# Gate and up weights of the experts read in runs of eight rows per partition, gathered x taken from every eighth column

## The reference, cut to what matters

```python
h = jax.nn.silu(jnp.einsum('td,edf->tef', xf, w_gate)) * jnp.einsum('td,edf->tef', xf, w_up)
y = jnp.einsum('tef,efd->td', h * gates[:, :, None].astype(h.dtype), w_down)
```

## Time and profile before

| | us |
|---|---|
| median of 3 runs | 989.9 (989.45 to 990.78) |
| the profiled execution, its own time | 992.38 |
| its span, first to last instruction | 990.7 |

### The profile page before, as it was taken

The page is one execution under the profiler, slowest core; times in us unless marked ns, Lnnn a source line. Parts: engine busy times, 40 slices in busy tenths (PEclk is TensorE's granted clock), DMA queues, the critical chain, the costliest instruction groups (busy, mean ns, idle before and its releaser), DMA issues.

```text
span 990.7 us, 14556 instructions
## 1 busy us (share of the span) xinstructions
PE 959.4 (97%) x5530; PEld 818.1 (83%) x5530; DVE 727.5 (73%) x905; ACT 561.3 (57%) x629; POOL 37.8 (4%) x79
## 2 busy tenths in 40 slices
PE   8999989999999999999999999899999999999997
PEld 7978988888888779878888788679887788888886
DVE  4888885988898774645988888756565977777566
ACT  3845652577777644563677667624553756656441
POOL 8000010100000000001000000000000000000010
PEclk9999998999999999999999999999999999999999
DMA  9833336299989945431599899745452566555711
GB/s 321 278 111 128 128 100 199 79 323 356 306 302 359 357 155 186 160 96 43 170 339 342 274 352 359 256 128 185 157 191 85 183 201 205 175 175 203 250 52 42
DMA packets 151985, 205.82 MB, mean 208 GB/s; under 512 B 6896, under 2 KB 123376, under 8 KB 151920
## 3 DMA queue, kind: packets, MB, share of 16 engines
q1 hardware_dynamic: 150912, 204.24, 61.4%
q10 hardware_dynamic: 1008, 0.71, 0.2%
HBM read 203.87 MB, written 1.05 MB: 207 GB/s over the span
## 4 chain that ended last, share of the span: by engine, by line
PE 79%; DVE 10%; issue 4%; ACT 4%; DMA 2%; SPq 1%; POOL 0%; POOLq 0%; DVEq 0%; ACTq 0%
PE psum L638 77%; DVE w_lo L1961 3%; ACT w_hi L1493 1%; ACT arena L1493 1%; DMA raw<-in_a_w_in 1%; DMA raw<-in_attn_w_in 1%; DVE stats L2225 1%; SPq L281 1%; DVE x_res L2245 1%; PE psum L1117 1%; DVE x_res L2238 1%; DVE xt L1978 0%; ACT mt_hi L1493 0%; PE psum L1368 0%; DVE mt_lo L1978 0%
## 5 line engine op out<-in xcount | busy, mean ns | idle before, releaser
L1961 DVE TENSOR_TENSOR w_lo<-raw,w_hi 128x2048 fp32r<-128x2048 f32 x184 | 418.1, 2287 | 71.6 <-ACT w_hi L1493 69.8
L1493 ACT ACTIVATE w_hi<-raw 128x2048 fp32r<-128x2048 f32 (+1 forms) x186 | 353.9, 1905 | 105.0 <-PE psum L638 43.7
L638 PE MATMUL psum<-xt,w_hi 128*128 128x256 f32 (+1 forms) x1056 | 253.6, 321 | 3.8 <-DVEq L2709 1.7
L638 PE MATMUL psum<-xt,w_lo 128*128 128x256 f32 x704 | 197.1, 280 | 0.0
L638 PEld LDWEIGHTS psum<-xt,w_hi 128*128 128x128 f32 x1056 | 177.1, 190 | 20.3 <-issue 2.7
L638 PE MATMUL psum<-w_hi,mt_hi 128*128 128x512 f32 (+1 forms) x448 | 174.1, 389 | 0.2 <-issue 0.2
L638 PE MATMUL psum<-w_hi,mt_lo 128*128 128x512 f32 (+1 forms) x448 | 171.3, 382 | 0.0
L638 PE MATMUL psum<-w_lo,mt_hi 128*128 128x512 f32 (+1 forms) x448 | 171.0, 382 | 0.0
L638 PEld LDWEIGHTS psum<-xt,w_lo 128*128 128x128 f32 x704 | 133.6, 190 | 0.0
L638 PE MATMUL psum<-w_hi,xt 128*128 128x512 f32 (+1 forms) x368 | 115.2, 385 | 8.0 <-ACT mem_v L1493 3.7
L638 PEld LDWEIGHTS psum<-w_hi,mt_lo 128*128 128x128 f32 x448 | 84.2, 188 | 16.7
(11 more groups left out here) (252 smaller groups left out, 1024.1 us busy)
## 6 DMA issues: line engine op xcount, KB each, us to landing
raw<-in_w_gate SPq DMA_DIRECT2D x64, 512.0 KB, 4.9
raw<-in_w_up SPq DMA_DIRECT2D x64, 512.0 KB, 6.1
raw<-in_w_down SPq DMA_DIRECT2D x64, 512.0 KB, 6.0
raw<-in_ffn_w_up SPq DMA_DIRECT2D x44, 512.0 KB, 4.6
raw<-in_a_w_in SPq DMA_DIRECT2D x26, 512.0 KB, 6.9
raw<-in_attn_w_in SPq DMA_DIRECT2D x24, 512.0 KB, 5.9
raw<-in_ffn_w_down SPq DMA_DIRECT2D x22, 512.0 KB, 4.0
raw<-in_w_o SPq DMA_DIRECT2D x16, 512.0 KB, 4.6
```

Source lines behind the costliest of these rows:

```text
L638: return pe.matmul(o, l, r, start=start, stop=stop, skip_group_check=skip)
L1493: return act.activation(o, i, f, **kw)
L1961: return dve.tensor_tensor(w_half(h, w_lo), w_half(h, raw), w_half(h, w_hi).bitcast(F32), ALU.subtract).then_inc(lo_split, 1)
```

## The change: what it does

It changes two things, which belong together. The view of the gate and up weights becomes `(p k)`: partition p now holds rows 8p to 8p + 7, and a half takes four of them, which lie side by side in memory, 4 KB of gate and 4 KB of up. The place in `raw` to which each row goes stays as it was (1 KB, then a gap of 1 KB). So chunk k now holds the rows k, k + 8, k + 16 and so on, and the stationary operand of the gather takes the same features: column k of each run of eight, 128 numbers of 4 bytes that lie 32 bytes apart, instead of 128 numbers side by side. The transposes in the branch `dense` change in the same way. Number, shapes and order of all instructions and all bytes moved stay the same.

```diff
-                wg = a["w_gate"][layer].rearrange("(g j) (k p) f -> g j p k f", j=PER_GROUP, p=P)
-                wu = a["w_up"][layer].rearrange("(g j) (k p) f -> g j p k f", j=PER_GROUP, p=P)
+                wg = a["w_gate"][layer].rearrange("(g j) (p k) f -> g j p k f", j=PER_GROUP, p=P)
+                wu = a["w_up"][layer].rearrange("(g j) (p k) f -> g j p k f", j=PER_GROUP, p=P)
...
+        def every_eighth(v, b, k):
+
+            return v[:, b, :].rearrange("p (m k) -> p k m", k=KC)[:, k, :]
...
-                                last = mm(o, x[:, b, P * k:P * k + P], perm[:, b, :],
+                                last = mm(o, every_eighth(x, b, k), perm[:, b, :],
...
-                            last = pe.transpose(again(b)[:, k // 4, k % 4, :], x_res[:, b, P * k:P * k + P], ident[:])
+                            last = pe.transpose(again(b)[:, k // 4, k % 4, :], every_eighth(x_res, b, k), ident[:])
```

## The result

| | before | after |
|---|---|---|
| first timing, median of four executions each, us | 989.81 | 1011.14 |
| ratio, 95% interval | | 1.0197 [1.0177, 1.0218] |
| the profiled execution, us | 992.38 | 1008.75 |
| its span, us | 990.7 | 1007.0 |

The four executions after took 1008.75, 1008.88, 1013.4 and 1913.76 us; the last one was disturbed and is left out of the ratio, but not of the median of four (the other three have their median at 1008.88). The change made the kernel 2.0% slower, from 1.8 to 2.2%. 1001.8 was forecast, with a range up to 1006.5.

What follows compares the result with a forecast made beforehand. TensorE was taken as the bound, DMA close behind with 1.4 us (4%) margin a group. Reads 0, gather +11.9, transposes 0 made 1002.6 on the span, 1001.8 us at the median; range 986.5 to 1006.5, the forecast's own 997 to 1006.5.

Steps and rivals of the forecast that it cites:

- The gather: Four gathers, 128 spread loads: 0.218 us each, between ends 0.109 and 0.458; +12.5 us, less 0.6 hidden, +11.9.
- some 300 was the sign named: Sign of being right: gather weight loads (tile perm over xt) near 0.3 us recorded instead of 0.19.
- two waits on `perm_t`: First gather of each layer: some 0.3 us of waiting hides part of the slower loads, twice 0.3.
- the 1.13 us of issue stays: Branch behind a layer's first gather: its 1.13 us of instruction issue follows the gather and isn't hidden.
- pass over the whole 4 KB: Upper end for a gather load: TensorE passes over all 4 KB, 0.458 us, +43.3 us; as rival 1033 us, chance 0.06.
- The line of 16 bytes: Gather loads, by the skill's SBUF cachelines: 0.229 us a load, some +14 us less 0.6; set beside the sum, not used.
- The read of gate and up weights, costed at 0: Expert weight transfers: packets stay 1 KB at 350 GB/s, cost 0; bounds from a 3.1 us gain to +9.6 us.
- a sign of being wrong: Expert groups of 37 us, with ScalarE waiting for w_up throughout, would show the forecast wrong.
- mirrored: Gate and up reads: 4 KB runs in memory only, taken to behave like runs in `raw` only, no gain.
- The witness itself: Third layer's up weights, 1 KB rows in memory, 4 KB runs in `raw`: 1 KB packets at 339 GB/s.
- The rival of slower transfers: Gate and up reads 8 KB apart fall under 330 GB/s; at 10% slower +9.6, 999.5 us with free loads; chance 0.05.
- The dense transposes, order and queues: Dense-branch transposes don't run, cost 0; SyncE issues the same DMAs after the same waits, group margin unchanged.

Runs made afterwards that it cites:

- e7: e4's dense reads with gate and up rows each in 4 KB runs in `raw`, gather as in the kernel before; 992.75 us, ratio 1.0006.
- e1: The kernel before with only the gather's spread weight loads, weights read as before (features don't match); 1005.38 us, ratio 1.0138.
- f1: e1 timed again, beside f2 and f3: the kernel before with the spread gather alone; 1006.23 us, ratio 1.0145.
- e5: The kernel before with its four gathers taking weights 8, 12, 16 and 20 bytes apart (sums changed), one execution; 1000.1 us.
- e2: The kernel before with only the `(p k)` reads of gate and up weights, gather as before (features don't match); 993.73 us, ratio 1.0021.
- e4: As e2, but a half takes rows 512 h + 4p to 4p + 3, so partitions' 4 KB runs join without holes; 991.02 us, ratio 0.9997.
- f4: The changed kernel with sorting moved into the `x_hi`/`x_lo` copies; gather reads neighbours, `start_sums` reads at 512-byte steps; 999.49 us, ratio 1.0075.
- f3: The whole changed kernel timed a third time, beside f1 and f2; 1009.35 us, ratio 1.0173 to the kernel before.
- f2: e2 timed again, beside f1 and f3: the kernel before with the `(p k)` reads alone; 995.02 us, ratio 1.0032.
- after_again: The changed kernel timed a second time, unaltered, beside the kernel before; 1008.72 us, ratio 1.0188.
- e3: e2 with gate rows and up rows each side by side in `raw`, so both transfer sides have 4 KB runs; 993.21 us, ratio 1.0025.

## Why the prediction was wrong

*What bounds it.* Right. TensorE's own time set the stage; e7 lets weights come earlier than before, and nothing is gained. That the DMAs are close behind was right as well, and it is what the cost of the reads comes from.

*The gather.* Right in mechanism, sign and place, short in size. The spread load was put at 0.218 us, the middle in ratio of two ends; it measures 0.245 (recorded 337 ns; some 300 was the sign named), so the term was 128 x 0.125 = +16.0 instead of +12.5. Taken off it was 0.6 for two waits on `perm_t`; the trace of before has only one of them, 0.3 us, and that went under as said. That "the 1.13 us of issue stays" failed: with the longer gather the issue behind it is hidden in the changed kernel, in both layers, 2.2 us (in e1 and f1 0.56 and 0.54 us of it are left). 16.0 - 0.3 - 2.2 = 13.5 us; the marks of the trace have 12.9, the ratios of e1 and f1 13.7 and 14.4. These errors together moved the sum by under 2 us. The upper end of that term, "pass over the whole 4 KB", falls with e5: the price stops rising at 16 bytes.

*The line of 16 bytes.* The sentence that the prediction set beside its sum gave 0.229 us a load and some +14 us. That was nearer than the middle of the two ends: measured are (7.73 - 0.40) / 31 = 0.236 at steps of 16 bytes and 0.245 at 32.

*The read of gate and up weights, costed at 0.* This is the step that failed. That packets stay at 1 KB was right (123376 both times). That the pace stays was not: gate and up move at 333 to 337 GB/s with the engines busy, where the kernel before has 349. In the prediction's own sum this makes a group 8 x 3.13 + 10.3 = 35.3 us of transfer, and the margin falls from 1.4 to 0.4 us, so that there is next to nothing to make up for a late half with. In the trace of the changed kernel one group without a gather took 37.08 us, the length that the text had named as a sign of being wrong. The argument was by piece length alone. That the case was "mirrored", so the same, was assumed and no row showed it. The witness itself was read rightly: the third layer's up weights lie a row of 5632 numbers (22.5 KB) apart from partition to partition, and by the measure given at e2 they move at 347 GB/s. So holes between the partitions are not dear as such. What differs in the changed kernel is a step of 8 KB and four pieces of a partition side by side in memory; of the two, e4 has the second alone and costs nothing. With a step of 8 KB between the partitions' runs and 1 KB pieces, w_up lands 0.2 to 0.8 us later than in the kernel before (f4 6.3, e2 6.5, f3 6.5, f2 6.6, after_again 6.6, after 6.9 against 6.1). It costs 2.1 us (e2) and 3.2 (f2), with long pieces 2.5 (e3), always with the gather as before; with a step of 4 KB no cost can be measured (e4, e7). The rival of slower transfers had the right place in it, with too large a size, a pace limit (under 330 GB/s) that was not needed for a cost, and a witness against it that did not bear on this case, and it was priced only with free loads, so that the range had no case with both. In the trace of the changed kernel the two are 12.9 + 3.4 = 16.3 us.

*The range.* Its top was a load of 0.25 us, hit almost exactly, with nothing for the reads. With the reads at half the upper bound that the text itself gave (+4.8) beside that load it would have reached 1011. The reads alone don't make up the whole miss of 9.3 us. On the profiled executions 1004.3 was forecast and 1008.75 came: 1.0 from the gather and 3.4 from the reads. The other 4.9 are scatter. The profiled execution of the kernel before stood 2.5 us above its median, while that of the changed kernel stood 2.4 under the median of four, which counts the disturbed one. All 13 undisturbed executions of the changed kernel (1007.2 to 1013.4) lie above the range, but it started from 989.9. From the later medians of the kernel before, 992.1 and 992.6, its top would have been 1008.7 to 1009.2, in the midst of them.

*The dense transposes, order and queues.* Cost nothing, as said: no form of them appears among the tile's rows, and the count of instructions on TensorE is the same 5530.

What stays open: why the step of 8 KB is slower, and one of 22.5 KB not. The runs tell the pattern from the piece length, not which part of the memory path pays, and the 32 register instructions go with it in every run. The packets are no longer on the mean, 51 ns for 1 KB in the expert stages of all twelve traces with short pieces; but those over 100 ns are 1.7 to 2.0% of them with the 8 KB steps and 0.9 to 1.1% without. Late weights vary from execution to execution (41.7, 34.1 and 31.4 us of waits for w_up in three traces of the changed kernel), and why is open too.

## What to carry to other kernels

A stationary operand whose numbers (4 bytes each) lie 16 bytes or more apart made the step of load and matmul twice as long here (0.245 against 0.120 us), so a layout of weights that looks better to the DMAs must not be paid by spread reads on the engine that binds; look first who would gain. If rows are to lie side by side per partition, let the partitions' runs join without holes (`(c p k)`, not `(p k)` read by halves): it won nothing over the old layout here, but it didn't cost what the steps of 8 KB did. When transfers fill 96% of a stage, a pace lower by 4% is not nothing. And when a range is drawn from two independent costs, one case in it must have both.

## What was not expected of the hardware

- A step of 20 bytes (7.48 us for 32 loads and matmuls) is a little cheaper than 16 (7.73) and 32 bytes (8.00); 12 bytes lies in between (5.89), 8 bytes is free (4.42).
- The moving side pays as well, though less by number: 512 numbers at steps of 512 bytes take (4.22 - 0.67) / 7 = 0.51 us instead of 0.229, 1.0 ns a number, where a spread load takes 0.245 / 128 = 1.9 ns.
- A copy that reads float32 at steps of 32 bytes takes 2167 ns instead of 1060 on ScalarE, and the subtraction 2095 instead of 1220 ns on VectorE.
- 4 KB pieces on both sides of a transfer cut the packets from 151985 to 102833; on one side alone they change nothing.
